# Moving three groups of transposes from inside one pair of weight chunks to the front of it, in the expert loop of a two-block kernel

## The chip, the cores and the metric

The kernel runs on one core of one Trainium2 chip. The metric is the device time of one execution in microseconds (us), lower is better. Times are medians of several runs; the profile is of one execution.

## The reference

The reference runs two transformer-like blocks over 512 tokens of width 1024. The first block is a gated convolution and a linear recurrence; the second is attention and then a mixture of 32 experts with top-4 routing. What the change touches is the expert layer of the second block:

```
def _clamped_swiglu(hgu):
    x_glu = jnp.minimum(hgu[..., ::2], SWIGLU_LIMIT)
    x_lin = jnp.clip(hgu[..., 1::2], -SWIGLU_LIMIT, SWIGLU_LIMIT)
    return x_glu * jax.nn.sigmoid(SWIGLU_ALPHA * x_glu) * (x_lin + 1.0)
...
    xs = h[tok]                                                        # tokens sorted by expert
    hgu = lax.ragged_dot(xs, w_gate_up, group_sizes) + b_gate_up[e_sorted]   # 1024 -> 2048
    act = _clamped_swiglu(hgu)                                               # 2048 -> 1024
    out = lax.ragged_dot(act, w_down, group_sizes) + b_down[e_sorted]        # 1024 -> 1024
    out = out * gates.reshape(-1)[order][:, None]
    return jax.ops.segment_sum(out, tok, num_segments=L)
```

Everything is float32.

## The kernel before

The expert layer is a loop over *items*. An item is up to 128 token rows that go to one expert; here there are 34 of them. Each engine runs its own program with a loop over the items, and the engines meet only through semaphores. An engine takes its instructions strictly in the order written, so a wait holds everything behind it on that engine.

**Weights.** An item reads 12 tiles of 1 MB (8 of `w_gate_up`, 4 of `w_down`) into six buffers, by DMAs that SyncE issues. A tile is two *chunks*, a *pair* `p` (0 to 11). Products have float32 precision out of two rounded parts: ScalarE writes the high part of each chunk (`split_high`, L1798, signal `hi_ready`), VectorE the remainder of a whole pair (`split_low`, L2542, signal `lo_ready`). Both parts have four slots, so that a chunk's slot is free once TensorE has used it (`hi_used`, `lo_used`). SyncE loads a new tile into a buffer when `lo_ready` says that the old one has been split.

**Products.** For each pair TensorE (`pair` and `product`, L979) does 12 matmuls of 128x512: for the first chunk two with the high part of the rows and two with their low part, the same for the second chunk, then four with the low part of the weights. Pairs 0 to 3 and 4 to 7 make the two halves of the gate/up result from the token rows `xTs`; pairs 8 to 11 make the output from the activation `aTs`, into banks 4 and 5.

**The activation.** When pair 7 is done, ScalarE does a Relu (L1804) and a Sigmoid (L1806) of the second half, VectorE clips the linear part (`clip_linear`, L2549), multiplies (`gate_part`, L2555) and finishes it (`activation`, L2561, signal `act_ready`). TensorE transposes the half in four 128x128 pieces (`turn`, L917, signal `at_ps`), ScalarE writes the high part of the transposed rows (`high`, L1772, signal `at_hi`), VectorE the low part (`low`, L2446, signal `at_lo`). Of the eight column blocks of `aTs`, pairs 8 and 9 use the first four, made from the first half, and pairs 10 and 11 the last four, made from the second half.

**The next item's rows.** GpSimd gathers the next item's token rows `xe` (L727) and signals `gathered`; TensorE transposes them in two groups of four (`xt_ps`), ScalarE and VectorE write high and low parts of `xTs` (`xt_hi`, `xt_lo`). TensorE waits for both low parts before the next item's pair 0, and GpSimd for the transposes before the next gather.

**Where these transposes stand before.** Inside pair 9, behind the four matmuls of its first chunk (`turns_within`: four of the activation's second half, eight of the next item's rows). VectorE's order around them is: `activation(1)`, `split_low(9)`, low part of the second half of `aTs`, `split_low(10)`, low part of the first half of `xTs`, `split_low(11)`, low part of the second half of `xTs`, and then `split_low(0)` of the next item.

Of the kernel before, what the change touches and what calls it, by code (L numbers as in the profile page):

```python
# [128 lines left out]
def program(nc, a, out, h1_dram, y_dram):  # L129
    slot_rows = nc.dram_tensor("slot_rows", (P * BLOCKS, 2), F32, kind="Internal").ap()  # L130
    slot_blocks = slot_rows.rearrange("(p b) w -> p b w", b=BLOCKS)
    with ExitStack() as ctx:
        sems = {}

        def sig(name):
            if name not in sems:
                sems[name] = ctx.enter_context(nc.semaphore(name))
            return sems[name]
# [11 lines left out]
        xTs = sb("xTs", [P, 2, KD, P], F32R)  # L150
# [151 lines left out]
        xe = m3.take(D)  # L302
        ysb = m3.take(D)
        actv = m3.take(D)
# [507 lines left out]
        def _(pe):  # L812
# [101 lines left out]
            def turn(x, bank):  # L914

                for k in range(4):
                    i = nc.tensor.transpose(ps[:, bank, k * P:(k + 1) * P], x[:, k * P:(k + 1) * P], IDENT)  # L917
                return i

            def experts(pe):  # L920
# [17 lines left out]
                for c in range(TC):  # L938
                    i = nc.tensor.transpose(ps[:, 5, c * P:(c + 1) * P], gm4[:, c, :], IDENT)
# [21 lines left out]
                for q in range(2):  # L961
                    i = mm(ps[:, 3, q * E:(q + 1) * E], evb[0:E, q, :], cst("ident", 0, E, E), start=True, stop=True)
# [10 lines left out]
                with pe.Fori(0, n_items) as i:  # L973

                    def product(c, banks, lhs, k, x_, w_, start, stop):

                        w = split[:, w_, c % SPLITS, :]
                        for q in range(2):
                            m = mm(ps[:, banks + q, :], lhs[:, x_, k, :], w[:, q * 512:(q + 1) * 512], start=start, stop=stop)  # L979
                        return m  # L980

                    def pair(p, banks, lhs, k, start, stop):

                        for n_ in range(2):
                            c = 2 * p + n_
                            pe.wait_ge(sig("hi_ready"), i * CHUNKS + (c + 1))
                            product(c, banks, lhs, k + n_, 0, 0, start and n_ == 0, False)
                            if p == 10 and n_ == 0:
                                pe.wait_ge(sig("at_lo"), i * 2 + 4)
                            product(c, banks, lhs, k + n_, 1, 0, False, False).then_inc(sig("hi_used"), 1)  # L990
                            if p == 9 and n_ == 0:
                                turns_within()
                        pe.wait_ge(sig("lo_ready"), i * PAIRS + (LEAD + p + 1))
                        product(2 * p, banks, lhs, k, 0, 1, False, False)
                        product(2 * p + 1, banks, lhs, k + 1, 0, 1, False, stop).then_inc(sig("lo_used"), 1)

                    def turns_within():

                        pe.wait_ge(sig("act_ready"), i * 2 + 2)
                        turn(actv[:, 512:1024], 6).then_inc(sig("at_ps"), 1)  # L1000
                        pe.wait_ge(sig("gathered"), i * 16 + 32)
                        turn(xe[:, 0:512], 7).then_inc(sig("xt_ps"), 1)
                        turn(xe[:, 512:1024], 1).then_inc(sig("xt_ps"), 1)

                    pe.wait_ge(sig("xt_lo"), i * 2 + 2)
                    for half in range(2):

                        pe.wait_ge(sig("lin_ready"), i * 2 + (half + 1))
                        if half == 1:
                            pe.wait_ge(sig("acc"), 2 * TC)  # L1010
                        for p in range(4):
                            if p == 1:
                                if half == 0:
                                    pe.wait_ge(sig("eo_ready"), i + 1)
                                for q in range(2):
                                    mm(ps[:, 2 * half + q, :], eo[:], bgu[:, half * D + q * 512:half * D + (q + 1) * 512], start=False, stop=False)  # L1016
                            if half == 1 and p == 2:

                                pe.wait_ge(sig("act_ready"), i * 2 + 1)
                                turn(actv[:, 0:512], 6).then_inc(sig("at_ps"), 1)  # L1020
                            pair(4 * half + p, 2 * half, xTs, 2 * p, p == 0, p == 3)
                    pe.wait_ge(sig("y_ready"), i + 1)
                    for p in range(4):
                        if p == 0:
                            pe.wait_ge(sig("at_lo"), i * 2 + 3)
                        if p == 2:
                            pe.wait_ge(sig("at_hi"), i * 2 + 2)
                        pair(8 + p, 4, aTs, 2 * p, p == 0, p == 3)

                def rows_so_far(t, lo, hi):  # L1030
# [77 lines left out]
            for n in range(1, N_IN):  # L1108
# [3 lines left out]
                if n in PLAIN:  # L1112
                    wait_tile(pe, T_IN + n)
                    w = tile(T_IN + n).rearrange("p (k n) -> p k n", k=KD)
                    for half in range(2):
                        for k in range(KD):
                            i = mm(dst[half], w[:, k, half * P:(half + 1) * P], hT[:, k, :], start=(k == 0), stop=(k == KD - 1))  # L1117
                        i.then_inc(sig("u_ready"), 1)
                else:
# [7 lines left out]
                    for half in range(2):  # L1127
                        for k in range(KD):
                            if n == PARTED[0] and half == 0:
                                pe.wait_ge(sig("hT_low"), k + 1)  # L1130
                            i = mm(dst[half], w[0][:, k, half * P:(half + 1) * P], hT_low[k], start=False, stop=(k == KD - 1))  # L1131
# [11 lines left out]
            for n in range(N_PW2):  # L1143
# [3 lines left out]
                for half in range(2):  # L1147
# [3 lines left out]
                    for k in range(KD):  # L1151
                        if m == 0:
                            pe.wait_ge(sig("v_pass"), 3 * KD + k + 1)
                        for w_, x_ in THREE:
                            i = mm(ps[:, m % 4, :], w[w_][:, k, half * P:(half + 1) * P], (vc_hi, vc_lo)[x_][k],  # L1155
                                   start=(k == 0 and (w_, x_) == (0, 0)), stop=(k == KD - 1 and (w_, x_) == (0, 1)))
# [3 lines left out]
            for n in range(N_OUT):  # L1160
# [17 lines left out]
                if n < N_OUT - 1:  # L1178
                    for kk in range(4):
                        for t in range(TC):  # L1180
                            i = out_product(t, kk)
                    i.then_inc(sig("out_used"), 1)
                else:
                    for t in range(TC):
                        for kk in range(4):
                            i = out_product(t, kk)
# [139 lines left out]
            for j in range(HM):  # L1326
                i = mm(ps[:, 3, j * META:(j + 1) * META], wkv[:, j * 256:j * 256 + P], kvanT[:, T:L], start=True, stop=True)
# [515 lines left out]
        def _(dve):  # L1843
# [600 lines left out]
            def low(x, q, bank, signal):  # L2444

                V.tensor_tensor(x[:, 1, 4 * q:4 * q + 4, :], ps[:, bank, :].rearrange("p (k n) -> p k n", k=4),  # L2446
                                x[:, 0, 4 * q:4 * q + 4, :], ALU.subtract).then_inc(signal, 1)
# [87 lines left out]
            with dve.Fori(0, n_items) as i:  # L2535

                def split_low(p):

                    s_ = slice(2 * p % SPLITS, 2 * p % SPLITS + 2)
                    dve.wait_ge(sig("hi_ready"), i * CHUNKS + (2 * p + 2))  # L2540
                    dve.wait_ge(sig("lo_used"), i * PAIRS + (p + 1))
                    V.tensor_tensor(split[:, 1, s_, :].rearrange("p a b -> p (a b)"), chunk_pair(p),  # L2542
                                    split[:, 0, s_, :].rearrange("p a b -> p (a b)"), ALU.subtract).then_inc(sig("lo_ready"), 1)

                def clip_linear(half):

                    dve.wait_ge(sig("glu_ready"), i * 2 + (half + 1))
                    gu = ps[:, 2 * half:2 * half + 2, :].rearrange("p b (n o) -> p (b n) o", o=2)
                    V.tensor_scalar(actv[:, half * 512:(half + 1) * 512], gu[:, :, 1], LIMIT, -LIMIT, ALU.min, ALU.max)  # L2549

                def gate_part(half):

                    gu = ps[:, 2 * half:2 * half + 2, :].rearrange("p b (n o) -> p (b n) o", o=2)
                    dve.wait_ge(sig("gsig_ready"), i * 2 + (half + 1))
                    V.scalar_tensor_tensor(gsig[:, half, :], gu[:, :, 0], LIMIT, gsig[:, half, :], ALU.min, ALU.mult).then_inc(sig("lin_ready"), 1)  # L2555

                def activation(half):

                    a_ = actv[:, half * 512:(half + 1) * 512]
                    dve.wait_ge(sig("lin_ready"), i * 2 + (half + 3))  # L2560
                    V.scalar_tensor_tensor(a_, a_, 1.0, gsig[:, half, :], ALU.add, ALU.mult).then_inc(sig("act_ready"), 1)  # L2561

                for p in range(4):
                    split_low(p)
                split_low(4)
                split_low(5)
                clip_linear(0)
                gate_part(0)
                activation(0)
                split_low(6)  # L2570
                split_low(7)
                dve.wait_ge(sig("at_hi"), i * 2 + 1)
                low(aTs, 0, 6, sig("at_lo"))
                split_low(8)
                clip_linear(1)
                gate_part(1)
                activation(1)
                split_low(9)
                dve.wait_ge(sig("at_hi"), i * 2 + 2)
                low(aTs, 1, 6, sig("at_lo"))  # L2580
                split_low(10)
                dve.wait_ge(sig("xt_hi"), i * 2 + 3)
                low(xTs, 0, 7, sig("xt_lo"))
                split_low(11)
                dve.wait_ge(sig("xt_hi"), i * 2 + 4)
                low(xTs, 1, 1, sig("xt_lo"))

            dve.wait_ge(sig("ln_rows_in"), 64)

# [121 lines left out]
```

## Time and profile before

| | |
|---|---|
| median of 3 runs | 1987.61 us (1987.07 to 1989.41) |
| the profiled execution | 1987.61 us, its span from the first to the last instruction 1985.9 us |
| TensorE matmul | busy 1933.1 us, 97% of the span, 8812 matmuls |
| VectorE | 1704.8 us, 86% |
| ScalarE | 1369.2 us, 69% |
| GpSimd | 458.9 us, 23% |
| mean granted TensorE clock | 0.984 |
| chain that ended last | TensorE 90%, of it the matmuls of L979 56% |

A time in the rows is in us from the start of the span unless it is marked ns. PE is TensorE's matmuls and PEld its weight loads, which run ahead of the matmul that they belong to; DVE is VectorE, ACT ScalarE, POOL GpSimd. In a timeline a row is a run of like instructions on one engine: start, time from the first start to the last end, engine, line, operation, what it writes and reads, how many, and in brackets how long the engine was idle before and what ended that. Ends of matmuls are modelled and overlap the next start, so that starts are compared with starts.

### The profile page before, as it was taken

How to read it: one execution, taken by the hardware profiler on the slowest of the kernel's cores; microseconds unless marked ns; L12 is line 12 of the kernel's file. 1: busy time of each engine (PE TensorE's matmuls, PEld its weight loads, DVE VectorE, ACT ScalarE, POOL GpSimd, SP SyncE). 2: the span in 40 equal slices, each digit the busy share in tenths (PEclk: the TensorE clock that was granted, in tenths of full speed). 3: DMA queues.
4: the chain of work that ended last, by engine and by line, in shares of the span. 5: the costliest groups of instructions: out<-in, count | busy, mean ns of one | idle time of the engine just before them, and what ended most of it. 6: DMA issues, size and time to landing. Idle time of an engine off the chain costs nothing.

```text
span 1985.9 us, 29677 instructions
## 1 busy us (share of the span) xinstructions
PE 1933.1 (97%) x8812; PEld 1543.3 (78%) x8812; DVE 1704.8 (86%) x1759; ACT 1369.2 (69%) x1742; POOL 458.9 (23%) x339
## 2 busy tenths in 40 slices
PE   6999999998989999999999999999999999999998
PEld 3657767786768887888888888888888888888886
DVE  6899977349765479999999999999999999999998
ACT  4456855224345526888888888888888888888885
POOL 6671000000000108223222232222322223222231
PEclk7999999999999988999999999999999999999999
DMA  8222225332010256999999999999999999999995
GB/s 317 80 106 85 85 95 181 129 95 86 22 43 23 64 170 260 382 388 385 368 382 368 387 376 368 388 373 389 372 375 384 363 382 375 372 386 364 387 370 213
DMA packets 152207, 533.04 MB, mean 268 GB/s; under 512 B 14479, under 2 KB 19759, under 8 KB 149408
## 3 DMA queue, kind: packets, MB, share of 16 engines
q1 hardware_dynamic: 136112, 492.45, 65.5%
q0 software_dynamic: 16048, 39.99, 7.9%
q8 instruction: 27, 0.44, 0.1%
q14 instruction: 20, 0.16, 0.0%
HBM read 517.75 MB, written 24.26 MB: 273 GB/s over the span
## 4 chain that ended last, share of the span: by engine, by line
PE 90%; DVE 7%; issue 1%; ACT 1%; DMA 1%; SPq 0%; DVEq 0%; ACTq 0%
PE ps L979 56%; PE ps L1126 4%; PE ps L1174 4%; PE ps L917 3%; PE ps L1117 3%; PE ps L1155 2%; PE ps L1131 2%; PE ps L1350 2%; PE ps L1222 2%; PE ps L885 2%; PE ps L1016 2%; PE ps L856 1%; PE ps L1104 1%; PE ps L870 1%; DVE arena L1934 1%
## 5 line engine op out<-in xcount | busy, mean ns | idle before, releaser
L979 PE MATMUL ps<-split,xTs 128*128 128x512 f32 x3264 | 770.7, 392 | 0.7 <-ACT split L1798 0.5
L979 PEld LDWEIGHTS ps<-split,xTs 128*128 128x128 f32 x3264 | 610.9, 188 | 130.8 <-DVE split L2542 1.3
L2542 DVE TENSOR_TENSOR split<-arena,split 128x2048 fp32r<-128x2048 f32 x204 | 466.6, 2287 | 45.6 <-ACT split L1798 45.6
L1798 ACT ACTIVATE split<-arena 128x1024 fp32r<-128x1024 f32 x408 | 409.8, 1054 | 101.2 <-PE ps L979 95.7
L2542 DVE TENSOR_TENSOR split<-ring,split 128x2048 fp32r<-128x2048 f32 x204 | 466.8, 2315 | 4.1 <-ACT split L1798 1.7
L1798 ACT ACTIVATE split<-ring 128x1024 fp32r<-128x1024 f32 x408 | 410.4, 1055 | 74.6 <-PE ps L979 35.4
L979 PE MATMUL ps<-split,aTs 128*128 128x512 f32 x1632 | 386.4, 392 | 0.5 <-DVE split L2542 0.5
L979 PEld LDWEIGHTS ps<-split,aTs 128*128 128x128 f32 x1632 | 303.4, 188 | 64.3 <-DVE split L2542 2.0
L727 POOL DMA_INDIRECT arena<-h_rows,slots x33 | 92.4, 2800 | 340.4 <-PE ps L917 246.4
L1960 DVE TENSOR_TENSOR split<-ring,split 128x2048 fp32r<-128x2048 f32 (+1 forms) x32 | 72.8, 2275 | 68.8 <-ACT split L1461 68.8
L775 POOL DMA_INDIRECT y_rows<-arena,slots x33 | 86.4, 2619 | 186.0 <-DMA arena<-h_rows,slots 125.7
L786 POOL DMA_DIRECT2D slots<-slot_rows x66 | 48.5, 735 | 316.7 <-issue 316.4
L1461 ACT ACTIVATE split<-ring 128x2048 fp32r<-128x2048 f32 (+1 forms) x32 | 60.7, 1897 | 70.7 <-PE ps L1174 49.5
L676 POOL TENSOR_TENSOR arena<-arena 128x512 f32<-128x512 f32 x55 | 74.6, 1356 | 27.8 <-ACT arena L1497 20.7
L917 PE MATMUL ps<-const,arena 128*128 128x128 f32 x552 | 72.4, 274 | 0.0
L917 PEld LDWEIGHTS ps<-const,arena 128*128 128x128 f32 x552 | 64.9, 141 | 9.0 <-DVE arena L2561 0.3
L456 POOL TENSOR_TENSOR eo<-const 128x128 fp32r (+1 forms) x34 | 66.7, 1961 | 21.3 <-issue 11.0
L1174 PE MATMUL ps<-split,arena_r 128*128 128x512 f32 x256 | 69.2, 391 | 0.0
L1934 DVE SCALAR_TENSOR_TENSOR ps<-arena,chan,ps 128x512 f32<-128x512 f32 x97 | 67.3, 751 | 0.9
L1126 PE MATMUL ps<-xTs,split 128*128 128x512 f32 x240 | 63.8, 408 | 0.3 <-DVE split L1960 0.3
L2549 DVE TENSOR_SCALAR arena<-ps 128x512 f32<-128x512 f32 x68 | 46.8, 688 | 18.5 <-ACT arena L1804 18.5
L1804 ACT ACTIVATE arena<-ps,small 128x512 f32<-128x512 f32 x68 | 46.1, 679 | 21.4 <-PE ps L979 21.3
(435 smaller groups left out, 2539.0 us busy)
## 6 DMA issues: line engine op xcount, KB each, us to landing
ring<-in_w_gate_up SPq DMA_DIRECT2D x170, 1024.0 KB, 8.7
arena<-in_w_gate_up SPq DMA_DIRECT2D x102, 1024.0 KB, 7.1
arena<-in_w_down SPq DMA_DIRECT2D x102, 1024.0 KB, 10.4
ring<-in_w_down SPq DMA_DIRECT2D x34, 1024.0 KB, 10.7
ring<-in_w_in SPq DMA_DIRECT2D x23, 1024.0 KB, 4.9
ring<-in_w_out SPq DMA_DIRECT2D x8, 1024.0 KB, 5.2
ring<-in_mod_w SPq DMA_DIRECT2D x10, 512.0 KB, 9.1
ring<-in_mod_w SPq DMA_DIRECT2D x4, 1024.0 KB, 4.9
```

What stands on the lines that cost most here:

```text
L456: return tt(eo[:], ident[:, bass.ds(e, 1)].to_broadcast([P, P]), ident[:, bass.ds(e + E, 1)].to_broadcast([P, P]), ALU.add).then_inc(sig(" ...
L676: G.tensor_tensor(vc[:, j, :], vc[:, j, :], tap_out[:, at % 4, :], ALU.add).then_inc(sig("tap_added"), 1)
L727: nc.gpsimd.indirect_dma_start(out=xe, out_offset=None, in_=h1_dram, in_offset=bass.IndirectOffsetOnAxis(rows, 0), bounds_check=last_token ...
L775: nc.gpsimd.indirect_dma_start(out=y_dram, out_offset=bass.IndirectOffsetOnAxis(idx_s, 0), in_=ysb, in_offset=None, bounds_check=last_row, ...
L917: i = nc.tensor.transpose(ps[:, bank, k * P:(k + 1) * P], x[:, k * P:(k + 1) * P], IDENT)
L979: m = mm(ps[:, banks + q, :], lhs[:, x_, k, :], w[:, q * 512:(q + 1) * 512], start=start, stop=stop)
L1126: mm(dst[half], w[w_][:, k, half * P:(half + 1) * P], hT_hi[k], start=(k == 0 and w_ == 0), stop=False)
L1174: i = mm(ps[:, 4 * half + t, :], src[x_][:, t * P:(t + 1) * P], w[w_][:, kk, :], start=(k == 0 and (x_, w_) == (0, 0)), stop=(k == 2 * KD ...
L1798: A(split[:, 0, c % SPLITS, :], chunk(c), ACT.Copy).then_inc(sig("hi_ready"), 1)
L1934: i = V.scalar_tensor_tensor(dst, src, w, acc, ALU.mult, ALU.add)
L1960: V.tensor_tensor(lo[:, c_], tile(ring_tile(s))[:, c_], hi[:, c_], ALU.subtract).then_inc(sig("w_lo"), 1)
L2542: V.tensor_tensor(split[:, 1, s_, :].rearrange("p a b -> p (a b)"), chunk_pair(p), split[:, 0, s_, :].rearrange("p a b -> p (a b)"), ALU.s ...
```

## The change

The transposes leave pair 9's inside and stand in front of it, with their two waits. The wait for the low part of `aTs`'s second half moves from the middle of pair 10 to its start, where it takes the place of the wait for the high part. On VectorE the low part of the second half of `xTs` moves ahead of `split_low(11)`. No instruction other than waits is added or removed, and no DMA is touched.

```
                             c = 2 * p + n_
                             pe.wait_ge(sig("hi_ready"), i * CHUNKS + (c + 1))
                             product(c, banks, lhs, k + n_, 0, 0, start and n_ == 0, False)
-                            if p == 10 and n_ == 0:
-                                pe.wait_ge(sig("at_lo"), i * 2 + 4)
                             product(c, banks, lhs, k + n_, 1, 0, False, False).then_inc(sig("hi_used"), 1)
-                            if p == 9 and n_ == 0:
-                                turns_within()
...
-                    def turns_within():
-
-                        pe.wait_ge(sig("act_ready"), i * 2 + 2)
-                        turn(actv[:, 512:1024], 6).then_inc(sig("at_ps"), 1)
-                        pe.wait_ge(sig("gathered"), i * 16 + 32)
-                        turn(xe[:, 0:512], 7).then_inc(sig("xt_ps"), 1)
-                        turn(xe[:, 512:1024], 1).then_inc(sig("xt_ps"), 1)
...
                     for p in range(4):
                         if p == 0:
                             pe.wait_ge(sig("at_lo"), i * 2 + 3)
+                        if p == 1:
+
+                            pe.wait_ge(sig("act_ready"), i * 2 + 2)
+                            turn(actv[:, 512:1024], 6).then_inc(sig("at_ps"), 1)
+                            pe.wait_ge(sig("gathered"), i * 16 + 32)
+                            turn(xe[:, 0:512], 7).then_inc(sig("xt_ps"), 1)
+                            turn(xe[:, 512:1024], 1).then_inc(sig("xt_ps"), 1)
                         if p == 2:
-                            pe.wait_ge(sig("at_hi"), i * 2 + 2)
+                            pe.wait_ge(sig("at_lo"), i * 2 + 4)
                         pair(8 + p, 4, aTs, 2 * p, p == 0, p == 3)
...
                 low(aTs, 1, 6, sig("at_lo"))
                 split_low(10)
-                dve.wait_ge(sig("xt_hi"), i * 2 + 3)
-                low(xTs, 0, 7, sig("xt_lo"))
+                for q in range(2):
+                    dve.wait_ge(sig("xt_hi"), i * 2 + 3 + q)
+                    low(xTs, q, 7 - 6 * q, sig("xt_lo"))
                 split_low(11)
-                dve.wait_ge(sig("xt_hi"), i * 2 + 4)
-                low(xTs, 1, 1, sig("xt_lo"))
```

## Rows read from the trace of the kernel before

**Rows 1.** The chain that ended last, in order of time, about one item.
```profile
1011.22 10.92 PE ps L979 x48
1022.60 2.75 PE ps L979 x12
1025.79 9.11 PE ps L979 x40
1036.20 10.04 PE ps L979 x44
1046.70 10.92 PE ps L979 x48
...
1933.70 10.92 PE ps L979 x48
```

**Rows 2.** Busy time by stretch: loop's first matmuls, item 0's end, a middle item.
```profile
core 0: us, PE busy (x) PEld busy (x) DVE busy (x) ACT busy (x) POOL busy (x), PEclk, DMA share, GB/s
753.19:758.50 5.31, 4.79 (x13) 3.29 (x12) 5.24 (x11) 4.57 (x7) 3.94 (x6) 0.50 0.01 0
780.00:797.27 17.27, 16.75 (x79) 13.12 (x78) 15.33 (x12) 14.05 (x17) 14.72 (x10) 1.00 1.03 404
1011.22:1046.70 35.48, 35.48 (x166) 29.43 (x165) 33.35 (x23) 29.49 (x34) 8.89 (x6) 1.00 1.02 380
```

**Rows 3.** Timeline of TensorE's weight loads, the down product of a middle item.
```profile
1030.88 3.59 PEld L979 LDWEIGHTS ps<-split,aTs 128*128 128x128 f32 x16
...
1034.51 1.46 PEld L917 LDWEIGHTS ps<-const,arena 128*128 128x128 f32 x12
...
1035.93 7.15 PEld L979 LDWEIGHTS ps<-split,aTs 128*128 128x128 f32 x32
...
1043.12 2.68 PEld L979 LDWEIGHTS ps<-split,xTs 128*128 128x128 f32 x12
```

**Rows 4.** Timeline of ScalarE and VectorE, the same item, up to the transposed rows.
```profile
1031.30 0.69 ACT L1804 ACTIVATE arena<-ps,small 128x512 f32<-128x512 f32 x1 [0.67 <-PE ps L979]
1032.02 0.72 ACT L1806 ACTIVATE arena<-arena,small 128x512 f32<-128x512 f32 x1
...
1032.65 2.94 ACT L1798 ACTIVATE split<-arena 128x1024 fp32r<-128x1024 f32 x3
1032.78 0.69 DVE L2555 SCALAR_TENSOR_TENSOR arena<-ps,arena 128x512 f32<-128x512 f32 x1
1033.51 0.69 DVE L2561 SCALAR_TENSOR_TENSOR arena<-arena 128x512 f32<-128x512 f32 x1
1034.12 2.29 DVE L2542 TENSOR_TENSOR split<-arena,split 128x2048 fp32r<-128x2048 f32 x1
...
1035.50 0.58 ACT L1772 ACTIVATE aTs<-ps 128x512 fp32r<-128x512 f32 x1
```

**Rows 5.** Timeline of VectorE, the same item, from there to the next item.
```profile
1036.32 0.69 DVE L2446 TENSOR_TENSOR aTs<-ps,aTs 128x512 fp32r<-128x512 f32 x1
...
1036.92 2.28 DVE L2542 TENSOR_TENSOR split<-arena,split 128x2048 fp32r<-128x2048 f32 x1
...
1039.12 0.69 DVE L2446 TENSOR_TENSOR xTs<-ps,xTs 128x512 fp32r<-128x512 f32 x1
...
1039.72 2.28 DVE L2542 TENSOR_TENSOR split<-arena,split 128x2048 fp32r<-128x2048 f32 x1
1041.92 0.68 DVE L2446 TENSOR_TENSOR xTs<-ps,xTs 128x512 fp32r<-128x512 f32 x1
...
1042.52 6.85 DVE L2542 TENSOR_TENSOR split<-ring,split 128x2048 fp32r<-128x2048 f32 x3
```

**Rows 6.** Timeline of item 0: its first matmuls, and its down product.
```profile
755.77 3.06 PEld L979 LDWEIGHTS ps<-split,xTs 128*128 128x128 f32 x8 [1.24 <-ACT split L1798]
...
784.14 0.69 DVE L2561 SCALAR_TENSOR_TENSOR arena<-arena 128x512 f32<-128x512 f32 x1
...
784.89 1.29 PEld L917 LDWEIGHTS ps<-const,arena 128*128 128x128 f32 x12 [0.29 <-DVE arena L2561]
...
790.64 2.60 PEld L979 LDWEIGHTS ps<-split,aTs 128*128 128x128 f32 x12 [0.94 <-DVE split L2542]
...
793.44 0.76 PEld L979 LDWEIGHTS ps<-split,aTs 128*128 128x128 f32 x4 [0.20 <-DVE split L2542]
```

## The prediction

> **What bounds the kernel now.** I began with the chain that ended last, in order of time [rows 1]. The reader is to see that in the expert loop it is TensorE and nothing else. One item repeats as 48, 12, 40 and 44 matmuls of L979 in 10.92, 2.75, 9.11 and 10.04 us, which is 0.2275 us a matmul whichever row one divides. Between those four rows are gaps of 0.46, 0.44, 1.30 and 0.46 us, each filled by other TensorE work: two bias matmuls, four transposes, twelve transposes, two bias matmuls. From 1011.22 to 1933.70 lie 26 items, so an item takes 922.48 / 26 = 35.48 us, and the sum of the rows and gaps is the same 35.48. There is no wait in it. The view of busy time by stretch says it again: TensorE is busy 35.48 of 35.48 us, its granted clock is 1.00 (2.4 GHz), while VectorE has 33.35 and ScalarE 29.49 [rows 2]. So nothing can be gained in an item except by fewer or quicker TensorE instructions, and the change has neither. What it can do is make TensorE wait, and since nothing else is on the chain, each such wait costs its full length in every item.
>
> The third view is the timeline of one item around the transposes, with start times on each engine [rows 3 to 5], because a wait that is met with time to spare leaves no mark in the sums; its margin must be read from starts. TensorE's weight loads are the thing to look at, since a wait holds the load first.
>
> **The transposes in front of pair 9.** Before: pair 8's first load is at 1030.88 and the first transpose's load at 1034.51, 16 matmuls later [rows 3]. The change takes four matmuls (pair 9's first chunk) from ahead of the transposes to behind them. TensorE then comes to the wait for the activation after 12 matmuls: 1030.88 + 12 x (3.63 / 16 = 0.227) = 1033.60.
>
> The activation is not ready then. It hangs on the end of pair 7, not on anything moved: Relu at 1031.30 (ScalarE sat idle 0.67 us for TensorE), Sigmoid at 1032.02, then on VectorE the product at 1032.78 and the last step at 1033.51 for 0.69 us, so to 1034.20 [rows 4]. How long TensorE needs to start after that is seen once, in item 0, where it did wait: the same VectorE step ended at 784.14 + 0.69 = 784.83 and the transpose's load started at 784.89 [rows 6], 0.06 us later. So the load goes at 1034.26 in place of 1033.60: TensorE stands still for **0.66 us** of each item. Before the change the same wait had 1034.51 - 1034.26 = 0.25 us to spare.
>
> Queued behind this wait are the twelve transposes, all of pair 9, and through `at_ps`, `xt_ps`, `hi_used` and `lo_used` the other engines. I followed what each gets late next, in the old item's times:
>
> - ScalarE's high part of `aTs` started at 1035.50, when its three chunks (1032.65 and 2.94 long) were done [rows 4]. The loads of all twelve transposes take 1.42 us (1034.51 to 1035.93, [rows 3]), four of them a third of that, so the four are done at about 1034.26 + 0.47, with an estimated 0.4 for the last one to run through, = 1035.1, before that. So it does not move.
> - `low` of the second half of `aTs` ends at 1036.32 + 0.69 = 1037.01 [rows 5]. The wait for it at the start of pair 10: pair 10's first load was 24 matmuls before 1043.12 [rows 3], at 1037.66, and is now at 1038.32. 1.3 us to spare; even without the shift it would have 0.6. The moved `at_lo` wait costs nothing, and dropping the `at_hi` wait gives nothing, as it was long met.
> - `split_low(9)` ends at 1036.41 [rows 4], pair 9's low matmuls now load at 1038.32 - 0.91 = 1037.41. To spare, 1.0.
> - Chunk 22's high part needs chunk 18's slot, now used in pair 9 behind the transposes, at about 1034.26 + 1.42 + 4 x 0.2275 + 0.3 (to run through) = 1036.9; ScalarE is busy until about 1035.50 + 3 x 0.5 = 1037.0 with the transposed parts. It hardly moves, and pair 11 needs it only at 1038.32 + 2.73 = 1041.05.
> - GpSimd's gather waits for the last transpose, which comes 0.25 us sooner. No DMA is issued by a moved instruction, and SyncE's loads of tiles follow `lo_ready`, treated next.
>
> **The order on VectorE.** From `activation(1)` on VectorE runs without a pause: 1034.12, 1036.32, 1036.92, 1039.12, 1039.72, 1041.92, 1042.52 [rows 4, 5]. A `split_low` takes 2.20 us start to start, a `low` 0.60. With the second `low` of `xTs` ahead, `split_low(11)` starts at 1040.32 and ends at 1042.60 in place of 1042.00, so with the 0.06 of above pair 11's last four matmuls may load at 1042.66. TensorE wants them at 1043.12 - 0.91 = 1042.21 by the old times, at 1042.87 by the times shifted by 0.66. So this wait has 0.21 us to spare behind the first one. By itself it would cost 1042.66 - 1042.21 = 0.45 us. The two don't add: both are reckoned from pair 7's end, and TensorE waits for the later. The gain of the new order, `xt_lo` complete at 1041.0 in place of 1042.60, is worth nothing, as pair 0 of the next item loads only at 1043.12. `split_low(0)` of the next item starts at 1042.52 in either order. SyncE's next tile is issued 0.60 us later against a TensorE that is 0.66 later.
>
> **Item 0** is different: its weights come late, and TensorE already waits there, 0.29 us for the activation, then for `split_low(10)` until 790.64 and for `split_low(11)` until 793.44 [rows 6]. The activation's wait grows to 0.29 + 0.91 = 1.20, but the four matmuls behind it then fill what was the wait before 790.64: 784.89 + 1.26 + 20 x 0.2275 = 790.70. Only the 0.60 us of the order on VectorE stays, of which some 0.1 is met again by the wait at the next item's start: I take 0.5.
>
> **Sum.** 33 x 0.66 + 0.5 = 22.3 us. The profiled execution's span is 1985.9 and 1.7 us lie around it; its 1987.61 is also the median. 1985.9 + 22.3 + 1.7 = **2009.9 us**, 1.1% slower. Bounds of the likeliest: the stall at least 0.60 (no time at all from VectorE to TensorE) and at most 0.76 (if `split_low(11)` came 0.3 later than I have it), so 33 x 0.60 + 0.3 = 20.1 to 33 x 0.76 + 0.6 = 25.7: 2007.7 to 2013.3; with the spread of the runs shown, 2006 to 2014.
>
> **The rivals.**
>
> *Given back downstream (not slower).* In item 0 most of a longer wait is swallowed by waits that TensorE would meet anyway. If the middle items had such waits behind the transposes, hidden because ends are modelled, the stall would only move them. It decides from the point where these waits reach 0.66 us an item; then 1987.6. For it speaks item 0. Against it, 44 matmuls in 10.04 us behind the transposes are 0.228 each, the same as 48 in 10.92 elsewhere [rows 1], so there is no wait to move. Chance 0.03, a third of that for a time below the old.
>
> *Only the order on VectorE costs.* If the activation's wait were met after all (it would have to be ready 0.66 us earlier), the wait for `split_low(11)` stands uncovered: 33 x 0.45 + 0.5 = 15.4, 2003.0 us. Against it stand the starts at 1033.51 and 784.89. Chance 0.03.
>
> *The two waits add.* If ScalarE's high part of `aTs`, and with it VectorE's tail, followed TensorE instead of its own queue, `split_low(11)` would slip with the stall: 33 x (0.66 + 0.45) + 0.5 = 37.1, 2024.7 us. It would take transposes that end 0.4 us later than I have them. Chance 0.04.
>
> *The clock falls.* A stall beside twelve transposes in every item could cost the granted clock. At a granted 0.50 (1.2 GHz) item 0's first eight loads are (3.06 - 0.19) / 7 = 0.41 us apart [rows 2, 6]. If the 36 matmuls behind the stall ran so, an item would lose 36 x (0.41 - 0.2275) = 6.6 us more, 34 items 223: about 2233 us. Against it: the end of item 0 has stalls of this size and the transposes, and was granted 1.00 [rows 2]. Chance 0.02. The Trainium skill, TensorE: Matmul & The Clock Gate, section A second HAM failure mode, tells of a kernel whose TensorE idled briefly between groups of matmuls and was moved between its two clocks for it, and its section Part 4: PE-mode transpose says that transposes do not count as work for the clock. By that rule the change would be dangerous; the trace of item 0 does not show it.
>
> **How the numbers follow.** The forecast itself has 0.88. The range must leave out no more than 2 in 10; 2006 to 2014 holds the likeliest's bounds and the run spread, and leaves out the rivals, 0.12 together, and some of the forecast's own error. A change under 0.2% (4 us) can't be told from none here. Slower: 0.88 + 0.03 + 0.04 + 0.02 = 0.97, rounded down to 0.96 for what I have not thought of; same 0.03, faster 0.01.
>
> **What the profile after would show.** In every item a bracket of about 0.66 us before the twelve transposes' loads, released by VectorE's last step of the activation; an item of 36.14 us in the chain, with VectorE (and ScalarE) steps in it where there was only TensorE; a chain row of 12 matmuls before the transposes and 48 or 36 + 12 behind; no wait before pair 11's last four; granted clock 1.00. I am wrong if there is no bracket at the transposes, if there is a second one released by `split` L2542 at pair 11, or if the item's period is not 35.48 plus the bracket.

## The result, and the profile after

The changed kernel takes 2003.93 us (median of 4, 2002.39 to 2006.63) against 1987.34 for the kernel before in the same runs. The ratio is 1.0081, with a 95% interval of 1.0068 to 1.0093: slower by 0.8%. The forecast was 2009.9 with a range of 2006 to 2014: the direction and the place of the loss were right, its size was not. The profiled execution's span is 2002.2 us against 1985.9.

The chain of the kernel after, in order of time, about one item. It answers to [rows 1].

```profile
1050.32 10.92 PE ps L979 x48
1061.70 2.75 PE ps L979 x12
1064.89 5.51 PE ps L979 x24
...
1070.42 0.70 ACT arena L1799
...
1072.62 0.70 DVE arena L2556
...
1073.37 1.53 PE ps L917 x12
1074.90 10.93 PE ps L979 x48
1086.29 10.92 PE ps L979 x48
```

Matmuls still go by at 0.2275 us each. But where 1025.79 to 1036.20 was one row of 40 matmuls and 1.30 us of transposes, the chain now leaves TensorE after 24, at 1070.40, runs over ScalarE and VectorE, and comes back to TensorE with the twelve transposes at 1073.37, 3.0 us later. (Pair 8's twelve matmuls run meanwhile and are off the chain.) An item is 1086.29 - 1050.32 = 35.97 us against 35.48. (From 906.42 to 1949.51, 29 items, it is 35.969.) The difference, 0.49 us, is the loss: 33 x 0.49 = 16.2 us of the 16.3 between the two spans.

The timeline of TensorE's weight loads and the engines around them, same kernel; it answers to [rows 3 to 5].

```profile
1034.01 2.68 PEld L979 LDWEIGHTS ps<-split,aTs 128*128 128x128 f32 x12
1034.44 0.69 ACT L1799 ACTIVATE arena<-ps,small 128x512 f32<-128x512 f32 x1 [0.67 <-PE ps L979]
...
1036.65 0.69 DVE L2556 SCALAR_TENSOR_TENSOR arena<-arena 128x512 f32<-128x512 f32 x1
...
1037.39 1.29 PEld L917 LDWEIGHTS ps<-const,arena 128*128 128x128 f32 x12 [0.69 <-DVE arena L2556]
1037.39 1.53 PE L917 MATMUL ps<-const,arena 128*128 128x128 f32 x12 [0.27 <-DVE arena L2556]
...
1038.65 8.05 PEld L979 LDWEIGHTS ps<-split,aTs 128*128 128x128 f32 x36
...
1043.45 2.28 DVE L2537 TENSOR_TENSOR split<-arena,split 128x2048 fp32r<-128x2048 f32 x1
...
1046.74 2.68 PEld L979 LDWEIGHTS ps<-split,xTs 128*128 128x128 f32 x12
```

The view of waits shows one waiting line for TensorE's loads between 800 and 1980 us:

```profile
PEld ps L917 <- DVE arena L2556: 23.0, 33, 0.7
```

So the predicted bracket is there, 0.69 to 0.70 us in 33 items, released by the activation's last step, 0.05 us after that step's end (1036.65 + 0.69 = 1037.34). And 23.0 us of it cost 16.3. The two numbers that differ are these: from pair 8's first load to the first transpose's load, 3.38 us, as forecast (2.72 + 0.66); from that load to the next item's first, 1046.74 - 1037.39 = 9.35 us, where I had 8.61 + 0.91 = 9.52. The 0.17 us is given back behind the wait. It lies in the transposes: from the first one's load to the load behind the twelfth it was 1034.51 to 1035.93, 1.42 us [rows 3], and is now 1037.39 to 1038.65, 1.26 us.

Of these, the gap between the first two loads holds the 0.17 us. These are single instructions, before and then after: the last 512-column matmul ahead of the transposes, the first transpose with its load, and the second transpose's load.

```profile
1034.50 0.39 PE L979 MATMUL ps<-split,aTs 128*128 128x512 f32 x1
1034.51 0.14 PEld L917 LDWEIGHTS ps<-const,arena 128*128 128x128 f32 x1
1034.73 0.27 PE L917 MATMUL ps<-const,arena 128*128 128x128 f32 x1
1034.74 0.14 PEld L917 LDWEIGHTS ps<-const,arena 128*128 128x128 f32 x1
```

```profile
1036.73 0.39 PE L979 MATMUL ps<-split,aTs 128*128 128x512 f32 x1
1037.39 0.14 PEld L917 LDWEIGHTS ps<-const,arena 128*128 128x128 f32 x1 [0.69 <-DVE arena L2556]
1037.39 0.33 PE L917 MATMUL ps<-const,arena 128*128 128x128 f32 x1 [0.27 <-DVE arena L2556]
1037.45 0.14 PEld L917 LDWEIGHTS ps<-const,arena 128*128 128x128 f32 x1
```

Without a wait the first transpose's load starts 0.22 us ahead of its matmul, while the 512-column matmul before it has its turn, and the second load comes 0.23 us after the first. After a wait the matmul starts with its load, and the second load follows after 0.06 us. So a delay of the load is not yet a delay of the matmuls. By the matmuls the account closes: from the last 512-column matmul to the first transpose it is 0.23 us before and 0.66 now, 0.43 more, and the first transpose's own record is 0.06 longer (0.33 against 0.27), together the 0.49 us of the item. (The brackets, 0.27 us for the matmuls and 0.69 for the loads, depend on where ends are put, and those of matmuls are modelled; neither is the loss itself. The loss is the period.)

A number of the result was at odds with this reading at first: one of the rivals, that only the order on VectorE costs, had forecast 2003.0 us, nearer to the median of 2003.93 than my own 2009.9. The trace shows no wait at pair 11, but it shows little room: `split_low(11)` ends at 1043.45 + 2.28 = 1045.73, and the loads that need it go at 1046.74 - 0.91 = 1045.83. Whether the loss had one cause, or half of it each, the experiments had to say.

### The profile page after: what moved, and what is told of

Read it like the earlier page. It is cut to its first block, busy times and chain, and to the rows that moved or that the text cites. A ratio compares the mean times of both kernels' runs of the same rounds, so it can differ in the third digit from the quotient of the medians.

```text
span 2002.2 us, 29677 instructions
## 1 busy us (share of the span) xinstructions
PE 1938.2 (97%) x8812; PEld 1540.7 (77%) x8812; DVE 1706.8 (85%) x1759; ACT 1370.1 (68%) x1742; POOL 393.5 (20%) x339
## 4 chain that ended last, share of the span: by engine, by line
PE 84%; DVE 9%; ACT 3%; issue 1%; DMA 1%; SPq 0%; DVEq 0%; ACTq 0%
PE ps L979 50%; PE ps L1121 4%; PE ps L1169 4%; PE ps L917 3%; PE ps L1112 3%; PE ps L1150 2%; PE ps L1126 2%; PE ps L1345 2%; PE ps L1217 2%; PE ps L885 2%; PE ps L1004 2%; PE ps L856 1%; ACT arena L1801 1%; ACT arena L1799 1%; DVE arena L2556 1%
## 5 line engine op out<-in xcount | busy, mean ns | idle before, releaser
L775 POOL DMA_INDIRECT y_rows<-arena,slots x33 | 69.5, 2105 | 269.4 <-issue 250.5
L786 POOL DMA_DIRECT2D slots<-slot_rows x66 | 54.9, 832 | 327.0 <-issue 321.3
L727 POOL DMA_INDIRECT arena<-h_rows,slots x33 | 39.4, 1193 | 326.1 <-PE ps L917 235.6
```

The lines of the kernel that those rows point to most:

```text
L775: nc.gpsimd.indirect_dma_start(out=y_dram, out_offset=bass.IndirectOffsetOnAxis(idx_s, 0), in_=ysb, in_offset=None, bounds_check=last_row, ...
```

## The experiments

All are compared with runs of the kernel before on the same chip: 1986.87 us beside the first four experiments, 1986.67 beside the last three. The edits are shown against the changed kernel, unless it is said otherwise. The period is that of an item, from the chain over 29 items. "Bracket" is the idle time before the loads. "By starts" is the bracket less the 0.04 us that lie between any two loads of 512-column matmuls without a wait.

**turns_only.** The change without VectorE's new order.

```
-                for q in range(2):
-                    dve.wait_ge(sig("xt_hi"), i * 2 + 3 + q)
-                    low(xTs, q, 7 - 6 * q, sig("xt_lo"))
+                dve.wait_ge(sig("xt_hi"), i * 2 + 3)
+                low(xTs, 0, 7, sig("xt_lo"))
                 split_low(11)
+                dve.wait_ge(sig("xt_hi"), i * 2 + 4)
+                low(xTs, 1, 1, sig("xt_lo"))
```

> The transposes moved in front of pair 9 as in the change, VectorE in its old order. My theory (A, the wait at the transposes is the whole cost): the profile of the change had a bracket of 0.69 us at the transposes' loads in each item but a period only 0.49 us longer, because the twelve loads then took 1.26 us and not 1.42 to the next load. So with VectorE's old order it should cost the same, 33 x 0.49 = 16 us over the kernel before, bracket 0.69, period 35.97. Rival (B, the cost is VectorE's order, split_low(11) coming late): little, 0 to 3 us. Rival (C, the two add in part): 33 x 0.45 or so, less than the change by a few us.

Measured: 2001.52 us, ratio 1.0075 (1.0061 to 1.0088), period 35.97. From the timeline of TensorE's loads:

```profile
1036.39 2.68 PEld L979 LDWEIGHTS ps<-split,aTs 128*128 128x128 f32 x12
1039.76 1.29 PEld L917 LDWEIGHTS ps<-const,arena 128*128 128x128 f32 x12 [0.69 <-DVE arena L2556]
1041.03 8.05 PEld L979 LDWEIGHTS ps<-split,aTs 128*128 128x128 f32 x36
```

The same bracket and the same period as the whole change. VectorE's new order adds nothing on top of the wait at the transposes. B falls by the time. C does not: its 33 x 0.45 = 14.9 us fits the 14.7 between the medians as well as A's 16 does, with runs that lie 5.3 us apart. It is the period, the same 0.49 us over 35.48 as in the change, that speaks against C.

**order_only.** VectorE's new order and the earlier `at_lo` wait, with the transposes where they were.

```
                             product(c, banks, lhs, k + n_, 1, 0, False, False).then_inc(sig("hi_used"), 1)
+                            if p == 9 and n_ == 0:
+                                pe.wait_ge(sig("act_ready"), i * 2 + 2)
+                                turn(actv[:, 512:1024], 6).then_inc(sig("at_ps"), 1)
...
-                        if p == 1:
-
-                            pe.wait_ge(sig("act_ready"), i * 2 + 2)
-                            turn(actv[:, 512:1024], 6).then_inc(sig("at_ps"), 1)
...
```

> The transposes stay in pair 9 where they were; VectorE's new order and the wait for the low part of aTs at the start of pair 10. A: this wait is met with 0.05 us to spare in the changed kernel only because TensorE is late there; uncovered it is 0.45 us by the loads' starts, so 33 x 0.4 to 0.45 + 0.5 = 14 to 15 us over the kernel before, with a bracket at pair 11's last four loads released by split_low. B: 16 us, the same as the change. If waits at a load are cheaper than their bracket in general (by some 0.17 us), it is 33 x 0.28 = 9 us.

Measured: 1999.06 us, ratio 1.0063 (1.0049 to 1.0077), period 35.86. Timeline of the loads:

```profile
1034.95 1.46 PEld L917 LDWEIGHTS ps<-const,arena 128*128 128x128 f32 x12
1036.38 6.25 PEld L979 LDWEIGHTS ps<-split,aTs 128*128 128x128 f32 x28
1043.10 0.76 PEld L979 LDWEIGHTS ps<-split,aTs 128*128 128x128 f32 x4 [0.47 <-DVE split L2536]
1043.90 2.71 PEld L979 LDWEIGHTS ps<-split,xTs 128*128 128x128 f32 x12
```

The second wait is real when nothing stands before it: bracket 0.47, cost 0.38 an item, 33 x 0.38 = 12.5 us. It lies between my 14 to 15 and the 9 that a fixed 0.17 off every wait would give. So the part that a wait gives back depends on where it stands: here, before a 512-column matmul, it is 0.05 of the 0.43 by starts. Why it is less than before transposes stays open. The transposes are in their old place, their loads take their old 1.42 us.

**two_earlier.** The transposes stand two matmuls earlier than in the kernel before, where the change has them four earlier. VectorE is in its old order.

```
                             product(c, banks, lhs, k + n_, 0, 0, start and n_ == 0, False)
+                            if p == 9 and n_ == 0:
+                                pe.wait_ge(sig("act_ready"), i * 2 + 2)
+                                turn(actv[:, 512:1024], 6).then_inc(sig("at_ps"), 1)
...
                             product(c, banks, lhs, k + n_, 1, 0, False, False).then_inc(sig("hi_used"), 1)
...
-                        if p == 1:
-
-                            pe.wait_ge(sig("act_ready"), i * 2 + 2)
-                            turn(actv[:, 512:1024], 6).then_inc(sig("at_ps"), 1)
...
```

> The transposes two matmuls earlier than in the kernel before (behind the first product of pair 9's first chunk, four matmuls' way being the change's). VectorE in its old order. By starts, the wait at the loads should be 0.66 - 2 x 0.2275 = 0.20 us. Theory L (a weight load normally runs ahead of its matmul by more than it needs, so the first 0.17 us of a wait before the transposes are free): period longer by 0.04, 1 us in all, so no change to be seen. Rival P (every part of the wait costs, and the 0.17 come from standing between two pairs rather than inside one): 33 x 0.20 = 6.8 us.

Measured: 1987.36 us, ratio 1.0003 (0.9994 to 1.0012), period 35.50.

```profile
1033.29 3.13 PEld L979 LDWEIGHTS ps<-split,aTs 128*128 128x128 f32 x14
1036.67 1.30 PEld L917 LDWEIGHTS ps<-const,arena 128*128 128x128 f32 x12 [0.24 <-DVE arena L2555]
1037.93 7.59 PEld L979 LDWEIGHTS ps<-split,aTs 128*128 128x128 f32 x34
```

This tells L (the first 0.17 us of a wait are free) from P (all of it costs) most clearly, 0.5 us measured against P's 6.8. A wait stands in each of the 33 items, 8.0 us in the view of waits, and it costs nothing that can be measured, 0.02 us an item. The loads behind it take 1.26 us, inside a pair as well as between two.

**rows_first.** As turns_only, the eight transposes of the next item's rows ahead of the activation's four.

```
+                            pe.wait_ge(sig("gathered"), i * 16 + 32)
+                            turn(xe[:, 0:512], 7).then_inc(sig("xt_ps"), 1)
+                            turn(xe[:, 512:1024], 1).then_inc(sig("xt_ps"), 1)
                             pe.wait_ge(sig("act_ready"), i * 2 + 2)
                             turn(actv[:, 512:1024], 6).then_inc(sig("at_ps"), 1)
-                            pe.wait_ge(sig("gathered"), i * 16 + 32)
-                            turn(xe[:, 0:512], 7).then_inc(sig("xt_ps"), 1)
-                            turn(xe[:, 512:1024], 1).then_inc(sig("xt_ps"), 1)
```

> As turns_only, but the eight transposes of the next item's rows come ahead of the four of the activation, so that they cover the wait: the activation's four then load at about 1033.6 + 0.23 + 7 x 0.11 = 1034.6 by the old item's times against 1034.26 when it is ready. A and L: no wait, 0 us against the kernel before, the twelve loads take 1.42 us again. P (0.17 us saved by the place between two pairs): period 35.31, 5.6 us faster than before.

Measured: 1987.30 us, ratio 1.0000 (0.9991 to 1.0009), period 35.48.

```profile
1064.58 2.68 PEld L979 LDWEIGHTS ps<-split,aTs 128*128 128x128 f32 x12
1067.30 1.46 PEld L917 LDWEIGHTS ps<-const,arena 128*128 128x128 f32 x12
1068.73 6.25 PEld L979 LDWEIGHTS ps<-split,aTs 128*128 128x128 f32 x28
```

The place in front of pair 9 costs nothing in itself and gives nothing: no bracket in the middle items, and 1.43 us again for the twelve. P's gain of 5.6 us is not there. The loss of the change is that what stands first there is not ready.

**in_pair8.** The transposes four matmuls earlier than in the change, behind pair 8's high products (`if p == 8 and n_ == 1` in `pair`), VectorE in its old order.

> The transposes stand four matmuls earlier than in the change, behind both chunks' high products of pair 8; VectorE in its old order. Theory L (the activation is ready at a time that pair 7 fixes, and the cost is the wait by the loads' starts less 0.17 us that the transposes run closer behind it): the wait by starts is 0.66 + 4 x 0.2275 = 1.57, bracket 1.60, period 35.48 + 1.40 = 36.88, in all 34 x 1.40 = 47 us over the kernel before. If a part of the wait is regained in proportion (0.49 of 0.66) and not as a fixed 0.17 us: 34 x 1.17 = 40 us.

Measured: 2033.79 us, ratio 1.0238 (1.0223 to 1.0254), which is 47 us more than before, period 36.87.

```profile
1076.12 1.77 PEld L979 LDWEIGHTS ps<-split,aTs 128*128 128x128 f32 x8
1079.49 1.29 PEld L917 LDWEIGHTS ps<-const,arena 128*128 128x128 f32 x12 [1.60 <-DVE arena L2555]
```

From pair 8's first load to the transposes' it is 3.37 us, as in the change and in two_earlier (3.38): pair 7's end sets this time wherever the transposes stand. The wait by starts is 1.56, the cost 1.39. What is given back before transposes is a fixed 0.17 us, not a share: a share would have made it 40 us.

**low_wait_only.** The kernel before with the `at_lo` wait at the start of pair 10 in place of `at_hi`.

> Only the wait for the low part of the second half of aTs goes from the middle of pair 10 to its start, in place of the wait for the high part; the rest is the kernel before. By the times the low part is ready 0.6 us before pair 10's first load: no bracket, 0 us. Any time it does cost would have to be taken from what I give to the order on VectorE.

Measured: 1987.31 us, ratio 1.0002 (0.9993 to 1.0011), period 35.48, no bracket. It costs nothing.

**rows_first_order.** The whole change with the next item's rows transposed first, as in rows_first.

> The change with the eight transposes of the next item's rows ahead of the four of the activation, and VectorE in its new order. No wait at the transposes, so the wait for split_low(11) is uncovered as in order_only: bracket 0.47 at pair 11's last four loads, period 35.86, 33 x 0.38 + 0.5 = 13 us over the kernel before. If the two costs of the change had been one and the same (both the activation's), 0 us.

Measured: 1999.03 us, ratio 1.0063 (1.0050 to 1.0077), period 35.83.

```profile
1071.39 1.46 PEld L917 LDWEIGHTS ps<-const,arena 128*128 128x128 f32 x12
1072.82 7.15 PEld L979 LDWEIGHTS ps<-split,aTs 128*128 128x128 f32 x32
1080.45 0.76 PEld L979 LDWEIGHTS ps<-split,aTs 128*128 128x128 f32 x4 [0.47 <-DVE split L2537]
```

Taking the first wait away brings the second one out, 0.35 us an item. To get back to 1987, the transposes' wait has to be covered or undone and VectorE's order undone as well.

All places of the transposes together, with what an item costs above 35.48:

| kernel | wait by loads' starts | bracket | cost |
|---|---|---|---|
| rows_first | none | none | 0.00 |
| two_earlier | 0.20, transposes | 0.24 | 0.02 |
| the change, turns_only | 0.65, transposes | 0.69 | 0.49 |
| in_pair8 | 1.56, transposes | 1.60 | 1.39 |
| order_only | 0.43, matmuls | 0.47 | 0.38 |
| rows_first_order | 0.43, matmuls | 0.47 | 0.35 |

## Why the prediction was right or wrong

*What bounds the kernel*: right. TensorE filled the item before, and no variant came under a period of 35.48.

*The activation is not ready after 12 matmuls*: right, with its place, its releaser and its 0.66 us at the loads; from pair 8's first load to the first transpose's it is 3.38 us as forecast, and in_pair8 and two_earlier confirm that this time doesn't move with the transposes.

*"TensorE stands still for 0.66 us of each item"*: this is the step that failed, and with it the sentence that each such wait "costs its full length in every item". The term 33 x 0.66 in the sum should have been 33 x 0.49; in two_earlier a wait of 0.20 us cost 0.02. I read the wait from the starts of the weight loads, where it shows, and took it for a delay of the matmuls, though a load normally starts 0.22 us ahead of its matmul and has that lead to lose. So I let the twelve transposes take the same time behind the wait as without one. The row that spoke against it stood in item 0 [rows 6]: there, behind a wait, I used 784.89 + 1.26 for the twelve, and 1.42 for the middle items, without asking why they differed. 33 x 0.17 = 5.6 us is nearly all of the error. My lower bound, 33 x 0.60, asked only how soon TensorE could start, not what it would save, so the range missed too. Of the signs of being wrong that I had named, the last one is met: the period is not 35.48 plus the bracket. The chain, too, has no row of 12 matmuls before the transposes, since it turns to ScalarE at pair 7's end; the row of 48 behind them is there.

*Item 0*: 0.5 us forecast. The spans leave 16.3 - 16.2 = 0.1 for everything outside the 33 items, so this term was some 0.4 us too high. The trace after has the wait before the transposes 1.47 us (forecast 1.20; the activation's last step started 0.26 later than in the profile before, 784.40 against 784.14) and the one at pair 11 0.57, and no wait at pair 10, as forecast:

```profile
785.14 1.29 PEld L917 LDWEIGHTS ps<-const,arena 128*128 128x128 f32 x12 [1.47 <-issue]
786.40 7.13 PEld L979 LDWEIGHTS ps<-split,aTs 128*128 128x128 f32 x32
794.10 0.76 PEld L979 LDWEIGHTS ps<-split,aTs 128*128 128x128 f32 x4 [0.57 <-DVE split L2537]
```

*The order on VectorE costs 0.45 by itself and nothing behind the first wait*: right in kind and nearly in size. By itself it was 0.38 (order_only); turns_only shows 0 of it in the change. The room of 0.21 us that I gave it was used up to about 0.05 by the 0.17 that TensorE regains. Had it regained more than 0.21, the second wait would have begun to take over.

*The moved `at_lo` wait and the dropped `at_hi` wait cost nothing*: right (low_wait_only). *ScalarE's high part does not move*: it started 4.6 us after pair 8's first load before (1030.88 to 1035.50) and after (1034.01 to 1038.64).

*The rivals*: "given back downstream" was right in a small part. Something is given back behind the wait, though not at a later wait and only 0.17 us; where the wait is no longer than that, as in two_earlier, it does end at "not slower". "Only the order costs" hit the time within 1 us and was wrong: with the order taken out, the loss stays. "The two add" was wrong: nothing was added, as the same period in turns_only and the change shows. The clock: the changed kernel's item was granted 1.00, as forecast, and no stall of these sizes changed it: in_pair8, with 1.60 us in each item, was granted 1.00 from 800 to 1980 us as well. The rule in the Trainium skill, TensorE: Matmul & The Clock Gate, sections A second HAM failure mode and Part 4: PE-mode transpose, does not show here:

```profile
1050.32:1086.29 35.97, 35.70 (x165) 29.36 (x165) 33.41 (x22) 29.49 (x34) 6.44 (x6) 1.00 1.01 369
```

The columns are those of [rows 2]. They hold a second warning: TensorE counts as busy 35.70 of 35.97 us, so the busy view shows 0.27 of the 0.49 that the item lost.

## What to carry to other kernels

On an engine that is never idle, moving a wait earlier costs from the point where its producer, followed back to where the time is really set, is no longer ready; here that point was 16 matmuls behind pair 7, less 0.25 us, and rearranging what else stands at the place (independent work first) removed it. The loss is to be reckoned in the period, not in the bracket of idle time: what runs ahead (weight loads) shows a longer wait than the matmuls behind it lose, and a wait of up to 0.2 us in front of short transposes was free. When a total agrees with a wrong theory, as 2003.9 us did with a forecast of 2003.0 here, only undoing one part at a time, and then reading the period, says which it was.

## What the runs showed of the hardware that I had not expected

Twelve 128-column transposes behind 512-column matmuls took 0.17 us less when TensorE had waited in front of them, in four kernels alike (the change, turns_only, two_earlier, in_pair8); before ordinary 512-column matmuls the gain was 0.05 to 0.08 us. The starts of single instructions show where the 0.17 us goes, from 0.23 to 0.06 us between the first two loads; what inside TensorE sets these two times no run here shows.

GpSimd's gather of the next rows (L727) took 2800 ns of the engine before and 1193 ns after, with the same 33 instructions:

```profile
L727 POOL DMA_INDIRECT arena<-h_rows,slots x33 | 92.4, 2800 | 340.4 <-PE ps L917 246.4
```

```profile
L727 POOL DMA_INDIRECT arena<-h_rows,slots x33 | 39.4, 1193 | 326.1 <-PE ps L917 235.6
```

It was 2754 to 2800 in the three kernels that have the transposes in their old place, 1130 to 1193 in four of the six that have them earlier, and 1514 and 1548 in the two that transpose the rows first. The timelines show what goes with it. These are the gather before, the gather after with the next `split_low`, and the gather of rows_first with the `split_low` that it starts in:

```profile
1037.17 2.98 POOL L727 DMA_INDIRECT arena<-h_rows,slots  x1 [10.64 <-PE ps L917]
```

```profile
1039.89 1.07 POOL L727 DMA_INDIRECT arena<-h_rows,slots  x1 [10.24 <-PE ps L917]
1040.06 2.28 DVE L2537 TENSOR_TENSOR split<-arena,split 128x2048 fp32r<-128x2048 f32 x1
```

```profile
1067.83 2.29 DVE L2537 TENSOR_TENSOR split<-arena,split 128x2048 fp32r<-128x2048 f32 x1
1069.52 1.52 POOL L727 DMA_INDIRECT arena<-h_rows,slots  x1 [9.29 <-PE ps L917]
```

Before, the gather starts 0.25 us after `split_low(10)` (1036.92 to 1039.20, [rows 5]) and ends 0.95 us behind its end. In rows_first it starts later in a `split_low` and ends 0.92 us behind its end. After the change it starts 0.17 us before `split_low(10)` and takes 1.07 us. That looks like a gather held until VectorE's running `split_low` is through, but spans on GpSimd are rough and no run tests it. GpSimd is off the path, so nothing came of it here.
